# A hybrid S5 / HGRN2 encoder on one core: real-factor products of the scans' level 0 as scaled copies on ScalarE

## The reference

```python
def s5_direction(u, lam_re, lam_im, log_step, b_re, b_im, c_re, c_im):
    ...
    lam_bar = jnp.exp(lam_dt)
    b_bar = ((lam_bar - 1.0) / lam)[..., None] * b
    ...
        bu = jnp.einsum('lbgh,gph->lbgp', u_blk.astype(jnp.complex64), b_bar)
        _, h_loc = lax.associative_scan(combine, (a_blk, bu), axis=0)
        h_all = h_loc + powers[:, None] * h[None]
        y = jnp.einsum('ghp,lbgp->lbgh', c, h_all).real

def s5_mixer(x, w_in, lam_re, ...):
    u = x @ w_in
    ...
    y = jnp.swapaxes((y_fw + y_bw).reshape(seq, bsz, MIX_WIDTH), 0, 1).astype(x.dtype) + d_skip * u
    y = jax.nn.gelu(y)
    y = y * jax.nn.sigmoid(y @ w_glu + b_glu)
    return y @ w_out
```

## Time and profile before

| | us |
|---|---|
| median of 3 runs | 2612.97 (2609.61 to 2614.67) |
| the profiled execution | 2607.99 |
| its span | 2606.2 |
| TensorE busy (matmuls) | 2477.1, 95% |
| VectorE busy | 1907.1, 73% |
| ScalarE busy | 899.6, 35% |
| GpSimd busy | 716.7, 28% |

### The profile page before, as it was taken

The page is one execution under the profiler, slowest core; times in us unless marked ns, Lnnn a source line. Parts: engine busy times, 40 slices in busy tenths (PEclk is TensorE's granted clock), DMA queues, the critical chain, the costliest instruction groups (busy, mean ns, idle before and its releaser), DMA issues. The chain is left out here.

```text
span 2606.2 us, 39853 instructions
## 1 busy us (share of the span) xinstructions
PE 2477.1 (95%) x12860; PEld 2072.2 (80%) x12860; DVE 1907.1 (73%) x3133; ACT 899.6 (35%) x1456; POOL 716.7 (28%) x553
## 2 busy tenths in 40 slices
PE   7787899999999999999999999997899999999997
PEld 5676778788888888878888888886687888887886
DVE  8899557778777768865666776666677777785887
ACT  3233342433333355422232223323124333333641
POOL 4798511333333400001111111112024333331000
PEclk9999899999999999999999999998999999999999
DMA  4334413166766697531101011000405667667863
GB/s 148 86 110 111 116 61 118 57 184 200 225 210 197 201 327 243 194 113 41 33 25 40 24 40 32 24 24 17 162 13 153 214 194 225 213 196 264 296 209 125
DMA packets 442289, 355.97 MB, mean 137 GB/s; under 512 B 30273, under 2 KB 376513, under 8 KB 438465
## 3 DMA queue, kind: packets, MB, share of 16 engines
q1 hardware_dynamic: 442176, 354.52, 43.6%
HBM read 296.31 MB, written 58.13 MB: 136 GB/s over the span
## 5 line engine op out<-in xcount | busy, mean ns | idle before, releaser
L2597 PE MATMUL ps<-aT_hi,w_hi 128*128 128x512 f32 x624 | 250.7, 402 | 4.3 <-DVE hg_q_raw L2876 2.5
L2547 POOL TENSOR_TENSOR w_lo<-w_raw_plain,w_hi 128x1024 fp32r<-128x1024 f32 x38 | 90.9, 2401 | 575.8 <-ACT w_hi L62 575.8
L2597 PE MATMUL ps<-aT_hi,w_lo 128*128 128x512 f32 x624 | 245.2, 393 | 0.0
L2597 PE MATMUL ps<-aT_lo,w_hi 128*128 128x512 f32 x624 | 243.8, 391 | 0.0
L625 PE MATMUL ps<-aT_hi,hgo_w_sets 128*128 128x512 f32 x640 | 202.8, 393 | 0.0
L625 PE MATMUL ps<-aT_hi,s5o_w_sets 128*128 128x512 f32 x640 | 202.8, 393 | 0.0
L1297 POOL TENSOR_TENSOR s5o_w_sets_plain<-s5o_w_sets_plain 128x512 f32<-128x512 f32 x80 | 112.3, 1405 | 213.4 <-DMA s5o_w_sets_plain<-in_ffn_w_in_dram 213.4
L1297 POOL TENSOR_TENSOR hgo_w_sets_plain<-hgo_w_sets_plain 128x512 f32<-128x512 f32 x80 | 111.4, 1394 | 212.0 <-DMA hgo_w_sets_plain<-in_ffn_w_in_dram 212.0
L625 PEld LDWEIGHTS ps<-aT_hi,hgo_w_sets 128*128 128x128 f32 x640 | 120.3, 188 | 26.4
L625 PEld LDWEIGHTS ps<-aT_hi,s5o_w_sets 128*128 128x128 f32 x640 | 120.2, 188 | 26.3
L2597 PEld LDWEIGHTS ps<-aT_hi,w_hi 128*128 128x128 f32 x624 | 117.4, 188 | 27.4 <-DVE hg_q_raw L2876 2.9
(11 more groups left out here) (445 smaller groups left out, 6191.8 us busy)
## 6 DMA issues: line engine op xcount, KB each, us to landing
s5o_w_sets_plain<-in_ffn_w_in_dram SPq DMA_DIRECT2D x168, 256.0 KB, 3.3
hgo_w_sets_plain<-in_ffn_w_in_dram SPq DMA_DIRECT2D x168, 256.0 KB, 3.3
w_raw_plain<-in_hg_w_in_dram SPq DMA_DIRECT2D x40, 512.0 KB, 4.0
aT_hi_plain<-in_ffn_w_out_dram SPq DMA_DIRECT2D x64, 256.0 KB, 4.5
s5o_w_sets_plain<-in_ffn_w_in_dram SPq DMA_DIRECT2D x96, 128.0 KB, 2.9
hgo_w_sets_plain<-in_ffn_w_in_dram SPq DMA_DIRECT2D x96, 128.0 KB, 2.8
s5o_hidden<-s5o_home_plain SPq DMA_DIRECT2D x11, 1024.0 KB, 6.6
hgo_hidden<-hgo_home_plain SPq DMA_DIRECT2D x11, 1024.0 KB, 6.9
```

What stands on the lines that cost most here:

```text
L2547: g.tensor_tensor(w_lo[b][:, :, :], w_raw[b][:, :, :], w_hi[b][:, :, :].bitcast(F32), ALU.subtract).then_inc(E[f"w_lo_done{b}"], 1)
L2597: ins = t.matmul(ps[:, half, :], w[b][:, kk, :], x[:, kk, cols], start=(kk == 0 and q == 0), stop=(kk == KT - 1 and q == 2))
```

## The change

For blocks 2 to 7 (SHARED = 2) the real-factor products of level 0, up and down, leave VectorE. ScalarE makes them as copies with a scale read per partition (`same_products`): four for each direction, 128x128 (128x126 down), from the state in PSUM into sc1 for the forward direction and into `row(n)` for the backward one. While ScalarE reads the forward banks, VectorE does cross and add2 of the backward ones (`halves_shared`); then they change sides, and last VectorE adds the two products. VectorE waits for the forward product before its forward `cross`, and for the backward product before its last add. ScalarE waits for all earlier steps of the scan (and, going up, for the inputs), and for VectorE's backward add2 before it reads the backward banks.

The position in ScalarE's order: the up pass at the head of block n, before `keep_kern_rows(n)`; the down pass immediately before `keep_state(n)`, behind `keep_u(n+2, (1,))`. For block 7, `split_y(3..5)` and `split_glu(1)` go from the end of block 6 to directly behind the up pass of block 7, and the down pass stands behind `split_y(6)`. The forward state may now be copied one step before the end of the scan, where it was three.

```diff
@@ -1436,8 +1436,25 @@
     INVERSE = LAM_READY + GJ - 1 + 4
     EXP, POW = 8, 18
     SCAN = 4 * (2 * LV - 1) + 2 * 4
-    SCAN_FW, SCAN_BW = SCAN - 3, SCAN
+    SHARED = 2
+    SCAN_LESS = 4
+
+    def scans_done(n):
+        return n * SCAN - SCAN_LESS * max(n - SHARED, 0)
+
+    def scan_fw(n):
+        return scans_done(n + 1) - (1 if n >= SHARED else 3)
     XT = 2 * NT
+
+    def scan_view(down, back):
+        m = NC // 2 - (1 if down else 0)
+        to = slice(2, None, 2) if down else slice(1, None, 2)
+        of = slice(1, 1 + (m - 1) * 2 + 1, 2) if down else slice(0, (m - 1) * 2 + 1, 2)
+        x = ps[:, 4 + 2 * back:6 + 2 * back, :].rearrange("p b (d q c) -> p (b d) q c", d=2, q=2)
+        return x, to, of, m
+
+    def same_view(n, back, m):
+        return (row(n) if back else sc1)[:, 0:PR * 2 * m].rearrange("p (d q c) -> p d q c", d=PR, q=2)
 
     def row(n):
         return h[:, n, :]
@@ -1943,6 +1960,19 @@
                 a.activation(kern_rows[:, L:2 * L - 1, :].rearrange("p a c -> p (a c)"), ps[:, 2, GRP:P],
                              ACT.Copy).then_inc(S["kern_rows_kept"], 1)
 
+            def same_products(n, down):
+                for back in range(2):
+                    if not down:
+                        a.wait_ge(S["in_done"], 4 * n + 2 * (back + 1))
+                    done = scans_done(n + 1) - 6 if down else scans_done(n)
+                    a.wait_ge(S["scan"], done + 2 * back)
+                    x, _, of, m = scan_view(down, back)
+                    for d in range(PR):
+                        col = n * DP + PR * back + d
+                        ins = a.activation(same_view(n, back, m)[:, d, :, :], x[:, d, :, of], ACT.Copy,
+                                           scale=k.mu[:, 0, 0, col:col + 1])
+                    ins.then_inc(S["same_down" if down else "same_up"], 1)
+
             def keep_state(n):
                 if n == 0:
                     a.wait_ge(S["pads"], 2)
@@ -1950,7 +1980,7 @@
                     a.wait_ge(S["out_done"], n)
                 for m in range(4):
                     if m % 2 == 0:
-                        a.wait_ge(S["scan"], n * SCAN + (SCAN_BW if m else SCAN_FW))
+                        a.wait_ge(S["scan"], scans_done(n + 1) if m else scan_fw(n))
                     a.activation(state[:, 2 * m:2 * m + 2, :, 1:NC + 1].rearrange("p a b c -> p (a b) c"),
                                  ps[:, 4 + m, :].rearrange("p (a c) -> p a c", c=NC), ACT.Copy
                                  ).then_inc(S["state_kept"], 1)
@@ -1990,7 +2020,7 @@
                     if n >= 1:
                         a.wait_ge(S["mixed"], 2 * n + half - 1)
                     else:
-                        a.wait_ge(S["scan"], KT * SCAN)
+                        a.wait_ge(S["scan"], scans_done(KT))
                     a.activation(gate[half][:, :], ps[:, GLU_BANKS[n % 4][half], :], ACT.Sigmoid,
                                  bias=k.glu_col[:, n:n + 1]).then_inc(S["gated"], 1)
 
@@ -2035,6 +2065,12 @@
                 if n == 2:
                     keep_u(3, (1,))
                     split_w(4)
+                if n >= SHARED:
+                    same_products(n, False)
+                if n == KT - 1:
+                    for kk in range(3, 6):
+                        split_y(kk)
+                    split_glu(1)
                 keep_kern_rows(n)
                 if n >= 2 and n + 2 < KT:
                     keep_u(n + 2, (0,))
@@ -2055,6 +2091,8 @@
                         split_y(kk)
                 if n == KT - 1:
                     split_glu(2)
+                if n >= SHARED and n < KT - 1:
+                    same_products(n, True)
                 if n < KT - 1:
                     keep_state(n)
                 if n >= 2 and n + 3 < KT:
@@ -2063,12 +2101,9 @@
                     gelu(n - 2)
                 if n >= KT - 2:
                     gelu(n - 1)
-                if n == KT - 2:
-                    for kk in range(3, 6):
-                        split_y(kk)
-                    split_glu(1)
                 if n == KT - 1:
                     split_y(6)
+                    same_products(n, True)
                     keep_state(n)
                     split_glu(3)
             keep_y(KT - 1)
@@ -2198,7 +2233,7 @@
                                 ).then_inc(S["kern_rows_done"], 1)
 
             def scan(n):
-                link = Steps(S["scan"], n * SCAN)
+                link = Steps(S["scan"], scans_done(n))
 
                 def steps(lv, down, dps):
                     d = 1 << lv
@@ -2244,6 +2279,28 @@
                     v.wait_ge(S["scan"], first)
                     return add2_b()
 
+                def halves_shared(down, ready, same_done):
+                    _, cross_f, _, add2_f = steps(0, down, slice(0, PR))
+                    _, cross_b, _, add2_b = steps(0, down, slice(PR, DP))
+                    ready()
+                    first = cross_b()
+                    v.wait_ge(S["scan"], first)
+                    first = add2_b()
+                    v.wait_ge(S["scan"], first)
+                    v.wait_ge(same_done, 2 * (n - SHARED) + 1)
+                    first = cross_f()
+                    v.wait_ge(S["scan"], first)
+                    first = add2_f()
+                    v.wait_ge(S["scan"], first)
+                    for back in range(2):
+                        if back:
+                            v.wait_ge(same_done, 2 * (n - SHARED) + 2)
+                        x, to, _, m = scan_view(down, back)
+                        v.tensor_tensor(x[:, :, :, to], x[:, :, :, to], same_view(n, back, m), ALU.add
+                                        ).then_inc(S["scan"], 1)
+                        last = link.step()
+                    return last
+
                 def whole(lv, down, last):
                     same, cross, add1, add2 = steps(lv, down, slice(0, DP))
                     v.wait_ge(S["scan"], last)
@@ -2254,7 +2311,11 @@
                     v.wait_ge(S["scan"], first)
                     return add2()
 
-                last = halves(False, lambda d: v.wait_ge(S["in_done"], 4 * n + 2 * (d + 1)))
+                inputs_in = lambda d: v.wait_ge(S["in_done"], 4 * n + 2 * (d + 1))
+                if n < SHARED:
+                    last = halves(False, inputs_in)
+                else:
+                    last = halves_shared(False, lambda: inputs_in(1), S["same_up"])
                 if n == 1:
                     turned_diagonal(0)
                 if n >= 2:
@@ -2266,9 +2327,12 @@
                 for lv in range(LV - 2, 0, -1):
                     last = whole(lv, True, last)
                 v.wait_ge(S["scan"], last)
-                last = halves(True, lambda d: None)
+                if n < SHARED:
+                    last = halves(True, lambda d: None)
+                else:
+                    last = halves_shared(True, lambda: None, S["same_down"])
                 v.wait_ge(S["scan"], last)
-                assert link.n == SCAN
+                assert link.n == scans_done(n + 1) - scans_done(n)
 
             v.memset(b_pair[:, :, :, :, :], 0.0).then_inc(S["pads"], 1)
             tables_to_rows()
```

More of the change, by code:

```diff
@@ L1427, in s5_gate_block @@
         "y_hi", "y_lo", "y_lo_last", "glu_loaded0", "glu_loaded1", "glu_hi0", "glu_hi1", "glu_lo0", "glu_lo1", "unit", "gated", "mixed", "early",
-        "row_free", "next_x_hi", "next_w_hi", "next_lo")}
+        "same_up", "same_down", "row_free", "next_x_hi", "next_w_hi", "next_lo")}
     u_scr, k_scr, y_scr = (nc.dram_tensor("s5_scratch_" + n, (P, c), F32, kind="Internal").ap()
```

## The result

The kernel with the change takes 2627.56 us (median; 2626.67 to 2628.09), the kernel before 2611.60 beside it: a ratio of 1.0061, 95% interval 1.0049 to 1.0073. It is 16 us slower. The forecast was 2630 with a range of 2617 to 2640. The profiled execution took 2628.09 us, span 2626.3; VectorE is busy 1895.9 us instead of 1907.1, ScalarE 926.3 instead of 899.6.

A forecast was written before the change was run, and what follows sets the result against it. VectorE's chain and TensorE's, through ScalarE's queue, were taken to bound the block loop together. 11.3 us (cycles to block 5) + 2.05 (scan 6) + 3.7 (tail) = 17 us more, from 2612.97 to 2630; range 2617 to 2640.

The forecast's parts named there:

- Two chains end together: Loop over blocks: VectorE's scan and TensorE's chain through ScalarE's queue finish together, 0.05 us apart at block 5.
- The place in the queue: Down pass, blocks 2 to 5: products behind `keep_u(n+2, (1,))` make the forward state copy start 3.5 us later.
- K(5): K(n) is when ScalarE starts `keep_state(n)`, behind `keep_u(n+2, (1,))`; for block 5 claimed 11.3 us later (8.8 to 16.3).
- One sign that I named: Blocks after each late state copy: `make_kern` on TensorE would be seen waiting for VectorE; no size given.
- Scan 6: VectorE's scan of block 6: lasts 22.45 us, was 24.8, but starts later; ends +2.05 us (1.6 to 3.2).
- Tail: Block 7, with its later start, moved splits and down products behind `gelu(6)`: +3.7 us (2.6 to 4.6).
- T(6): Moment VectorE ends the scan of block 6, 270.74 us in the kernel before; block 7's times count from it.
- The sum: Whole kernel: 11.3 + 2.05 + 3.7 = 17 us more (13 to 24).
- Up pass at nothing: Up passes, blocks 3 to 6: ScalarE's products cost nothing, fitting where it waited anyway; block 2's lateness moves nothing.
- Faster: Rival for the loop: VectorE alone paces it and ScalarE is always in time; gains 14 us, 2599; chance 0.08.
- Heavier: Rival: TensorE keeps half clock through the 24 products behind `make_kern` too; 27 us in all, 2640; chance 0.09.
- Slowing each other in PSUM: Rival: VectorE and ScalarE in PSUM at once slow each other; held by the products' upper bound, no chance of its own.

The follow-up runs named there:

- this part alone: Kernel before the change plus only the shared down pass of blocks 2 to 5, at the change's place in ScalarE's queue: 2625.80 us, ratio 1.0061.
- GpSimd's relief: Kernel before the change, with block 7's forward `make_cl` moved from GpSimd to VectorE and row 6's low part from VectorE to GpSimd: 2609.76 us, ratio 0.9995.
- both edits together: Changed kernel with down products of blocks 2 to 5 ahead of `keep_u(n+2, (1,))` and block 7's splits back ahead of its up pass: 2611.20 us, ratio 0.9999.

## Why the prediction was right

**Two chains end together.** Right, and the whole of the result hangs on it. The VectorE reading alone gave 2599; nothing like it came, not even with the products at the better place (2611.20), because behind VectorE and TensorE stood GpSimd as a third, which the 2599 left out.

**The place in the queue.** Right in cause (whole change 1.0061, this part alone 1.0061, one place earlier 0.9999) and in size: 3.5 us forecast for the state copy, 3.45 measured; `make_kern` at K + 9.9 forecast, at 9.5, 10.0, 10.5 and 10.8 in blocks 3 to 6 (163.24 - 153.78 at block 3, 263.75 - 252.98 at block 6); K(5) 11.3 us later forecast, 11.2 measured. Part of that closeness is luck: each copy starts 0.25 us behind the one ahead and not 0.29, and the half clock cost more than I put in. One sign that I named failed in most blocks: `make_kern` was to wait for VectorE, and it did so only in block 3, by 0.19 us; in blocks 4 to 6 the slow `start_state` ended last.

**Scan 6.** +2.05 forecast (1.6 to 3.2), +3.2 measured. Its length was right (22.6 us for 22.45); it started at K(5) + 10.9 and not + 9.9. The mis-sized term is `start_state(6)`, 6.64 us, half clock nearly all through, where I had taken it for part of it only.

**Tail.** +3.7 forecast (2.6 to 4.6), +2.4 measured, outside these bounds. `start_state(7)` took 5.53 us instead of 6.53, so the row that `gelu(6)` waits for came sooner. The forward products of the last down pass were ready at T(6) + 28.4 (313.84 and 1.1 us) and not at + 30, and scan 7 ended at + 31.3 and not + 32.7. The cause was wrong in one point as well. I gave 1.5 of these us to the splits of rows 3 to 5; putting them back gained nothing. What holds block 7 is the DMA, `gelu(6)` and the down products in a row. My sum had that chain too, and its end at + 34.0 against + 30.3 (measured + 32.6) is the whole of the 3.7 us, whatever the splits do: the 1.5 us was a part of the same wait, taken earlier, and not a cost of its own.

**The sum.** 17 us forecast, 16.0 measured between the medians. Scan 6 was too small by 1.2 us and the tail too large by 1.3, and they cancel: that is luck. The three cycles carry 11.2 us of it.

**Up pass at nothing.** Right: with the up passes alone the ratio is 0.9996. VectorE does wait 6.88 us in the up pass of block 2, and it costs nothing: K(2) is 153.78 us in the changed kernel and 153.57 where only the down passes are shared.

**The rivals.** Faster: fell, by the two kernels with the early down products (0.9999 each), although VectorE's work did get 11 us less. Heavier: the half clock did not reach the 24 products behind `make_kern`; they took 5.77 to 5.78 us in the changed kernel's blocks 3 to 5, 0.24 us each, where the gate's products at the full clock take 0.23. The half clock did come at other products that no rival named, those of the gate behind the long wait for GpSimd. Slowing each other in PSUM: VectorE's operations beside a scaled copy took 0.68 to 0.70 us, against 0.68 and 0.69 in the earlier trace rows. The Trainium skill (PSUM — Partial Sum Buffer, Specifications), by which both engines have the full bandwidth on different banks, agrees with that.

## What to carry to other kernels

Handing work to an idle engine costs by the place in its queue, not by the engine's busy share: ScalarE was busy a third of the time, and still 2 us of copies in each of four passes cost 16 us where they stood behind a wait for TensorE. Before moving work, list what the receiving engine waits for just ahead of that place and when that wait ends, and compare it with the moment at which the result is wanted; if there is a choice, put the work ahead of the long wait. And when an engine is relieved and nothing moves, look for the chain that ended at the same time: here shared products (0.9999) and GpSimd's relief (0.9995) were each worth nothing, and together 0.25% (0.9975).

## What the runs showed of the hardware

Copies of 128x126 or 128x128 from PSUM with a stride of two and a scale read per partition start 0.25 us apart on ScalarE (four in 1.13 us), less than the 0.29 worked out from the earlier trace rows. The Trainium skill's figures (ScalarE: Activation LUTs, What ACT_TABLE_LOAD costs) give an estimated 0.29 us apart too; the trace has less.

An idle of 4.7 us was followed by the 1.2 GHz level each time, but the time that the same 64 products then took was different from block to block (5.08, 5.85, 6.38, 6.64 us); with 2.98 us of idle the clock held at one block (3.71 us) and fell at three (5.35, 5.22 and 5.38). At the gate's products it was 1.00 behind 1.46 us of idle and fell to 0.50 behind 2.85, 2.95 (0.51 there) and 3.34 us. And it does not fall alike in two executions: behind two short waits, 1.57 and 0.31 us, it was 0.50 at 176 to 178 us with both edits together; behind 1.60 and 0.31 us, with the early down products alone, it was 1.00. K(2) to K(3) took 29.7 us in the first case and 28.1 in the second.
